# Experts of a MoE layer: three quarters of down in high and low parts, slots eight partitions apart, 8 KB weight pieces, three buffers for stored rows

## The reference

```python
idx, gw = route(h1)                  # 8 of 64 experts for each token, and their weights
for each expert e, rows = its tokens:         # 4352 rows over 64 experts, 68 on average
    h = silu(h1[rows] @ w_gate[e]) * (h1[rows] @ w_up[e])    # (n, 1024) @ (1024, 256)
    y = (h @ w_down[e]) * gate_weight                        # (n, 256) @ (256, 1024)
out = layer_norm(ALPHA * h1 + shared_swiglu(h1) + sum over a token's 8 experts of y)
```

## Time and profile before

| | |
|---|---|
| median of three runs | 1628.31 us (1626.76 to 1630.15) |
| profiled execution, whole | 1625.87 us |
| its span, first to last instruction | 1624.0 us |
| granted TensorE clock, mean over the span | 0.954 |
| busy: PE / DVE / ACT / POOL | 92% / 62% / 37% / 21% |
| bytes read from HBM and written | 301.33 MB and 42.12 MB |

### The profile page before, as it was taken

How to read it: one execution, slowest core, us unless ns; L and a number is a source line. 1 busy time by engine, 2 the same in 40 slices (tenths; PEclk the granted TensorE clock), 3 DMA queues, 4 the chain that set the end, 5 groups by cost and what they waited for, 6 DMA issues and landing times. The chain is left out here.

```text
span 1624.0 us, 20669 instructions
## 1 busy us (share of the span) xinstructions
PE 1494.0 (92%) x7986; PEld 1119.5 (69%) x7990; DVE 1006.1 (62%) x1713; ACT 601.9 (37%) x880; POOL 335.4 (21%) x233
## 2 busy tenths in 40 slices
PE   7999999979989985999997999999999999999654
PEld 6999999968888874444343777777766666677321
DVE  5649777245567664144554777777777777777276
ACT  3665333240230220000003555555555555555101
POOL 0000000022224221021230233333332221121024
PEclk9999999979999996999998999999999999999885
DMA  5222222200000002700074899999999999997392
GB/s 204 66 69 90 90 91 77 67 14 1 1 1 1 1 2 84 327 14 14 14 270 165 332 370 379 367 370 371 372 368 363 361 362 367 365 368 311 141 399 87
DMA packets 53159, 313.21 MB, mean 193 GB/s; under 512 B 14928, under 2 KB 15952, under 8 KB 34320
## 3 DMA queue, kind: packets, MB, share of 16 engines
q1 hardware_dynamic: 33312, 276.16, 44.6%
q0 software_dynamic: 19760, 35.89, 6.0%
HBM read 301.33 MB, written 42.12 MB: 211 GB/s over the span
## 5 line engine op out<-in xcount | busy, mean ns | idle before, releaser
L1880 DVE TENSOR_TENSOR gate_up_lo<-wide,gate_up_hi 128x2048 fp32r<-128x2048 f32 x128 | 293.1, 2291 | 92.2 <-ACT gate_up_hi L1823 91.6
L1823 ACT ACTIVATE gate_up_hi<-wide 128x2048 fp32r<-128x2048 f32 x128 | 244.6, 1913 | 7.4 <-PEq L1219 7.4
L302 PE MATMUL bank<-x_hi,w_hi 128*128 128x274 f32 x768 | 223.9, 291 | 0.0
L304 PE MATMUL bank<-x_hi,w_lo 128*128 128x274 f32 x768 | 223.0, 290 | 0.0
L303 PE MATMUL bank<-x_lo,w_hi 128*128 128x274 f32 x768 | 222.0, 289 | 0.0
L1751 PE MATMUL bank<-gate_up_hi,rows_hi 128*128 128x512 f32 x512 | 206.3, 403 | 7.7 <-DVE rows_lo L1889 7.7
L1753 PE MATMUL bank<-gate_up_hi,rows_lo 128*128 128x512 f32 x512 | 201.1, 393 | 0.0
L1752 PE MATMUL bank<-gate_up_lo,rows_hi 128*128 128x512 f32 x512 | 200.2, 391 | 0.0
L1689 POOL DMA_INDIRECT expert_rows<-lru,slot_ids x64 | 117.9, 1843 | 326.1 <-DVE lru L1896 312.5
L1771 PE MATMUL bank<-wide,zt 128*128 128x512 f32 x344 | 154.8, 593 | 1.0 <-DVE zt L1916 1.0
L302 PEld LDWEIGHTS bank<-x_hi,w_hi 128*128 128x128 f32 x768 | 144.9, 189 | 0.8 <-issue 0.5
(11 more groups left out here) (280 smaller groups left out, 2367.1 us busy)
## 6 DMA issues: line engine op xcount, KB each, us to landing
wide<-in_w_exp SPq DMA_DIRECT2D x64, 2048.0 KB
wide<-in_w_exp SPq DMA_DIRECT2D x43, 1024.0 KB, 12.8
w_raw<-in_w_in SPq DMA_DIRECT2D x48, 512.0 KB, 3.3
last_down<-in_w_exp SPq DMA_DIRECT2D x21, 1024.0 KB
expert_rows<-expert_rows SPq DMA_DIRECT2D x8, 2048.0 KB, 13.9
wide<-in_w_out SPq DMA_DIRECT2D x1, 3584.0 KB, 22.0
wide<-in_w_out SPq DMA_DIRECT2D x1, 2560.0 KB, 12.5
zt<-in_x_t SPq DMA_DIRECT2D x2, 1096.0 KB, 8.4
```

What stands on the lines that cost most here:

```text
L302: nc.tensor.matmul(out, wh[:, k, :], x_hi[:, k, at], start=(k == 0), stop=False)
L304: last = nc.tensor.matmul(out, wl[:, k, :], x_hi[:, k, at], start=False, stop=(k == DC - 1))
L1823: nc.scalar.activation(half(w_hi[b % 2], u), half(w_gu[b % RAW], u), ACT.Copy).then_inc(s_whi, 1)
L1880: nc.vector.tensor_tensor(half(w_lo[b % 2], u), half(w_gu[b % RAW], u), half(w_hi[b % 2], u), ALU.subtract).then_inc(s_wlo, 1)
```

## The change

Five edits. (1) Three of the four (row chunk, column half) units of down, `DN_UNITS`, are multiplied in parts; the fourth stays plain float32. For it hidden is split as well. Down is loaded as 1536 columns (6 KB a partition, two buffers) and 512 columns (2 KB, three buffers). ScalarE now writes both halves of y. (2) Rank 16i + g of an expert goes to partition 8g + i (`RANKS_APART` = 8), and `mem.ids` is read by eight DMAs. (3) The weights lie in HBM as two arrays; gate_up comes as two pieces of 8 KB for each partition, in one DMA. (4) y has three buffers. (5) The first expert's gate_up is split in quarters, with the rows' parts between them. Besides, constants that only the delta rule needs are a tensor of their own, which makes room. The core of the diff:

```diff
@@ loads @@
-    sp.dma_start(mem.w_gu[i], expert[:, 0:W_GU]).then_inc(mem.gu_loaded[i], 16)
-    sp.dma_start(mem.w_dn[i], expert[:, W_GU:W_EXP].rearrange("p (c n) -> p c n", c=FC)).then_inc(mem.dn_loaded[i], 16)
+DN_UNITS = ((0, 0), (0, 1), (1, 0))
+def load_gate_up(sp, mem, dram, b):
+    sp.dma_start(mem.w_gu[b % RAW].rearrange("p (h n) -> p h n", h=2), dram["w_gu"][b].rearrange("h p n -> p h n"))\
+        .then_inc(mem.gu_loaded[b % RAW], 16)
+def load_down(sp, mem, dram, b):
+    sp.dma_start(mem.w_dn[b % DN_RAW], dram["w_dn"][b, :, 0:DN_SPLIT]).then_inc(mem.dn_loaded[b % DN_RAW], 16)
+def load_down_whole(sp, mem, dram, b):
+    sp.dma_start(mem.w_dn_whole[b % RAW], dram["w_dn"][b, :, DN_SPLIT:]).then_inc(mem.dn_whole_loaded[b % RAW], 16)
@@ slots, in mixing_stage @@
-            pool.dma_start(mem.ids[:, :], dram["slots"].rearrange("(c p e) w -> c p (e w)", p=P, e=NE)[0])\
-                .then_inc(s_ids, 16)
+            by_rank = dram["slots"].rearrange("(c i g e) w -> c i g (e w)", i=RANKS_APART, g=P // RANKS_APART, e=NE)
+            for i in range(RANKS_APART):
+                pool.dma_start(mem.ids[i::RANKS_APART, :], by_rank[0, i]).then_inc(s_ids, 16)
@@ SyncE @@
-            for b in range(RAW - 2, NE):
-                if RAW <= b + 2 < NE:
-                    sp.wait_ge(s_wlo, 2 * (b + 2 - RAW) + 2)
+            gate_up(RAW)
+            gate_up(RAW + 1)
+            for b in range(DN_RAW, NE):
+                sp.wait_ge(s_dlo, b - DN_RAW + 1)
+                load_down(sp, mem, dram, b)
                 if b >= RAW:
                     sp.wait_ge(s_dn1, b - RAW + 1)
+                    load_down_whole(sp, mem, dram, b)
+                gate_up(b + RAW)
@@ TensorE, down @@
                     for c in range(FC):
-                        last = nc.tensor.matmul(mem.bank[4 + n][:, :], hidden_t[:, c, :],
+                        if (c, n) in DN_UNITS:
+                            unit = DN_UNITS.index((c, n))
+                            at = slice(512 * unit, 512 * unit + 512)
+                            nc.tensor.matmul(out, h_hi[:, c, :], d_hi[:, at], start=(c == 0), stop=False)
+                            nc.tensor.matmul(out, h_hi[:, c, :], d_lo[:, at], start=False, stop=False)
+                            last = nc.tensor.matmul(out, h_lo[:, c, :], d_hi[:, at], start=False, stop=(c == FC - 1))
+                        else:
+                            last = nc.tensor.matmul(out, hidden_t[:, c, :], w_dn_whole[b % RAW], start=False, stop=True)
@@ ScalarE, end of its loop @@
                 if b:
                     write_y(b - 1)
+                act.wait_ge(s_hdt, b + 1)
+                nc.scalar.activation(h_hi, mem.bank[6][:, 0:FC * P].rearrange("p (c i) -> p c i", c=FC), ACT.Copy)\
+                    .then_inc(s_hhi, 1)
+                split_down(b)
                 split(b + 2, 1)
@@ VectorE, its loop @@
                 split_rows(b + 1)
+                split(b + 1, 1)
                 split(b + 2, 0)
-                if b:
-                    write_y(b - 1)
-                dve.wait_ge(s_hdt, b + 1)
-                split(b + 2, 1)
+                split_hidden(b)
+                split_down(b)
```

More of the change, by code:

```diff
@@ L62 @@
 BIG = 1e30
+ROUTING = 2 * P + 2 + 5 * NE + NE * TILES + 2
 LEVELS = 7
@@ L67 @@
 _at = 0
-for _name, _n in (("ident", P), ("tri", P), ("before", P), ("ones", P), ("masks", LEVELS * P), ("future", P),
-                  ("experts", NE), ("valid", TILES + 1), ("row", 1), ("ln_eps", 1), ("over", TILES + 1),
+for _name, _n in (("ident", P), ("tri", P), ("before", P), ("ones", P), ("experts", NE), ("valid", TILES + 1), ("row", 1), ("ln_eps", 1), ("over", TILES + 1),
                   ("entries", (TILES + 1) * TOPK * 4)):
@@ L1187, in take @@
             nonlocal at
-            view = mem.carve(mem.states, at, *dims)
+            view = mem.carve(mem.routing, at, *dims)
             at += int(np.prod(dims))
@@ L1617, in expert_stage @@
         rows = mem.rows
-        act_g, hidden = (carve(mem.zt, D * ROWS + FF * i, FF) for i in range(2))
-        hidden_t = carve(mem.zt, D * ROWS + 2 * FF, FC, P)
-        y = [carve(mem.lru, D * i, D) for i in range(2)]
-        x_t = carve(mem.lru, 2 * D, DC, P)
+        y = [carve(mem.lru, D * i, D) for i in range(Y_ROWS)]
+        act_g, hidden = (carve(mem.lru, D * Y_ROWS + FF * i, FF) for i in range(2))
+        hidden_t = carve(mem.lru, D * Y_ROWS + 2 * FF, FC, P)
+        x_t = carve(rows[1], 0, DC, P)
+        h_hi, h_lo = (take(f"hidden_{n}", FC, P, dt=F32R) for n in ("hi", "lo"))
+        d_hi, d_lo = (take(f"down_{n}", DN_SPLIT, dt=F32R) for n in ("hi", "lo"))
         extra_ids = ctx.enter_context(nc.sbuf_tensor("extra_ids", [P, 4], U32))
@@ L1708, in _ @@
                 gather(b + 2 * ROWS)
-            for i in range(2):
-                pool.wait_ge(s_out[i], 16 * (NE // 2))
+            for i in range(Y_ROWS):
+                pool.wait_ge(s_out[i], 16 * len(range(i, NE, Y_ROWS)))
             pool.sem_inc(s_xfree, 1)
             def extra(i):
-                pool.wait_ge(s_xload, i * 48 + 48)
+                pool.wait_ge(s_xload, i * 64 + 64)
                 pool.sem_inc(mem.passed, 1)
@@ L1747, in up @@
                 for k in range(DC):
-                    if k % 4 == 0:
-                        pe.wait_ge(s_wlo, 2 * b + k // 4 + 1)
+                    if b == 0 and k % 2 == 0:
+                        pe.wait_ge(s_wlo, k // 2 + 1)
+                    elif k % 4 == 0:
+                        pe.wait_ge(s_wlo, splits(b - 1) + k // 4 + 1)
                     at = slice(512 * k, 512 * k + 512)
@@ L1807, in extra @@
                     for c in range(FC):
-                        last = nc.tensor.matmul(mem.bank[4 + n][:, :], hidden_t[:, c, :],
-                                                w_dn[0][:, c, 512 * n:512 * n + 512], start=(c == 0), stop=(c == FC - 1))
+                        unit = FC * c + n
+                        weights = w_dn[0][:, 512 * unit:512 * unit + 512] if (c, n) in DN_UNITS else w_dn_whole[0]
+                        last = nc.tensor.matmul(mem.bank[4 + n][:, :], hidden_t[:, c, :], weights,
+                                                start=(c == 0), stop=(c == FC - 1))
                 last.then_inc(s_xdn, 1)
@@ L2087, in constant_tables @@
 def constant_tables():
-    c = np.zeros((P, N_CONSTS), np.float32)
+    c, d = np.zeros((P, N_CONSTS), np.float32), np.zeros((P, N_DELTA_CONSTS), np.float32)
     def put(name, value):
-        at, n = CONSTS[name]
-        c[:, at:at + n] = value
+        table, out = (CONSTS, c) if name in CONSTS else (DELTA_CONSTS, d)
+        at, n = table[name]
+        out[:, at:at + n] = value
     p, q = np.arange(P)[:, None], np.arange(P)[None, :]
```

153 lines of the change are left out of this document (95 added, 58 removed).

## The result

The changed kernel takes 1641.12 us (median of 4 runs, 1637.68 to 1642.3), the kernel before 1628.27 in the same comparison (4 runs, 1626.76 to 1630.15): a ratio of 1.0077, 95% interval 1.0065 to 1.009. It is slower by 12.9 us, where 8 us less were forecast, and the time lies outside the range of 1592 to 1632. The profiled execution took 1642.30 us, with a span of 1640.5.

A forecast was written before the change was run, and what follows sets the result against it. TensorE bounded the old kernel; the busiest DMA engines would bound the new. First new gate_up load 879.8 + 7 + 60 S, then 25.5 and 2.5, gave 1517.8 against 1525.26: -7.5 us, 1618.4 profiled, 1620 us median, range 1592 to 1632.

The forecast's parts named there:

- The bound: Expert stage: it moves from TensorE, 9.49 us an expert after the change, to the busiest DMA engines.
- The compute side: Expert stage: TensorE's period falls to 9.49 us, ScalarE needs 8.2 and VectorE 8.4 us, and nothing is late.
- The first rival: Rows spread over all 16 DMA engines, S = 8.97, TensorE stays the bound at 9.49 us: 1594 us, chance 0.20.
- S: Time of the busiest DMA engines for one expert: between 9.83 (packet estimate) and 10.17 us (landings), taken as 10.05.
- 8 KB pieces: Gate_up rows as two packets, down rows as 6 KB and 2 KB: bytes cost the same, no capacity added.
- The 2.5 us at the end: Loss priced at the stage's end, since rows now unsent when the last weights land would be sent before them.
- Slots eight apart: New slot layout: again eight engines with 8 rows each at 64 tokens, the busiest holding as much as before.
- The lead: gate_up's time from issue to read falls from 22.6 to 16.0 us; landings of 15 us just fit.
- the slower rival: Shorter lead: landings over 16 us stop ScalarE and engines run dry; 1635 us at S = 10.3, chance 0.15.
- Three y buffers: ScalarE's waits for a stored y vanish; worth nothing, since its idle time hid them from TensorE.
- The start: First expert in quarters: first up near 876.2, 3.7 us sooner, mostly not kept; eight slot-table reads cost nothing.
- theory G: From the follow-up runs: faster compute engines, or their more SBUF reads and writes, slow the loads; 1622 to 1628 with down plain.

The follow-up runs named there:

- a_apart4: The changed kernel with slots of an expert four partitions apart in place of eight: 1593.21 us, ratio 0.9794.
- b_dn62: The kernel before with down loaded by two DMAs, 6 KB and 2 KB a partition, in place of one: 1626.03 us, ratio 0.9997.
- a_p16: The changed kernel with gate_up stored and loaded as one 16 KB piece for each partition again: 1639.99 us, ratio 1.0079.
- b_p8: The kernel before with gate_up as two 8 KB pieces for each partition in one DMA: 1626.93 us, ratio 1.0.
- a_gu_late: The changed kernel with each gate_up load issued one down load later, about 5 us later in the period: 1664.01 us, ratio 1.0229.
- b_dn62_late: The kernel before with down in 6 and 2 KB and each gate_up issued right behind the down load, 5.4 us later: 1631.27 us, ratio 1.0029.
- a_gu_early: The changed kernel with gate_up's second low half split ahead of the rows' low parts on VectorE, releasing the next load earlier: 1637.15 us, ratio 1.0062.
- a_y2: The changed kernel with two buffers for stored rows in place of three: 1641.48 us, ratio 1.0093.
- a_apart1: The changed kernel with slots as before the change, rank r in partition r: 1649.33 us, ratio 1.0131.
- a_four: The changed kernel with all four units of down in parts, down loaded in one 8 KB piece, slots eight apart: 1639.29 us, ratio 1.0069.
- a_four_apart4: The changed kernel with all four units of down in parts, down in one 8 KB piece, and slots four apart: 1584.31 us, ratio 0.9717.

## Why the prediction failed, point by point

**The bound was named rightly.** That it moves from TensorE to the eight DMA engines that carry rows, and that slots eight apart leave them eight, is shown by a_apart4: only the slots differ, and the pace goes from 10.23 to 9.46, with TensorE at 100.

**The compute side was right.** TensorE's period of 9.49 is a_apart4's 9.46; ScalarE's 8.2 us is 0.824 x 9.46 = 7.8 there, VectorE's 8.4 is 0.871 x 9.46 = 8.2. Nothing was late. The first rival's 1594 is what a_apart4 takes, 1593.21; it needed the rows spread, which eight apart does not do.

**The step that failed is S, "I take 10.05".** By landings it was 10.40, above both bounds (9.83 and 10.17). Put into the sum of the prediction against the profile:

| term | predicted | measured |
|---|---|---|
| first new gate_up load | 879.8 | 882.52 |
| 7 + 60 S | 610.0 | 631.0 (to 1513.5) |
| last landing to the end of the last down | 28.0 | 29.1 |
| end of the last down | 1517.8 | 1542.6 |

Of 24.8 us, 21.0 are S, 2.7 the start and 1.1 the chain behind the last landing. The profiled execution came 23.9 above the 1618.4 forecast for it. Both bounds were taken from the bytes or from the old kernel's landings, as if the time of an expert's loads were a property of the loads. It is not: 10.02 or less in b_dn62, 10.17 in the kernel before, 10.40 here. And 10.17 was a mean over a growth that slows: in windows of 100 us from 900 on, the old kernel's down loads land after 8.8, 11.2, 12.6, 14.3 and 15.4 us.

With S = 10.40 the sum of the prediction gives 1620 + 60 x 0.35 = 1641 us, the measured median. That it fits so closely is luck in part: the 3.8 us of the other two terms are made up by the profiled execution, which lies 1.2 us above its median here and lay 2.4 below it before.

**8 KB pieces** at nothing in capacity: right (a_p16, b_p8). The 2.5 us at the end cannot be told apart in the 29.1.

**Slots eight apart, "the busiest engines hold as much as before"**: wrong in size. In the kernel they are worth 8 us (1649.33 to 1641.12), and the growth of the old kernel's landings falls from 7.4 us to 2.8. A likely reason, argued and not shown: before, the first 36 rows of an expert already fill one engine with eight of them (partitions 0 to 3 and 32 to 35); eight apart, that takes 53 (ranks 0, 4, 16, 20 and so on to 52), so that with fewer tokens the busiest engine has less.

**The lead, "while a backlog exists no engine idles"**: not safe to rely on. The issue came as I walked it: 10.5 us after the start of an up (1204.13, the up at 1193.59), against 10.1 forecast and 4.67 before. Landings of 20.1 us are over the 16.0 of lead, and ScalarE waits as the slower rival said; it gave 1635 at S = 10.3, and should have had the larger chance. But that this later issue is what raised S is argued and not shown. 5 us more cost another 0.33 us an expert (a_gu_late), and a late issue brought back growing landings in the old kernel (b_dn62_late); both put gate_up within 1.3 us of down, where the changed kernel keeps 4.3 us, nearly the old 4.6. And issuing it earlier gave 0.03 to 0.05 us an expert (a_gu_early).

**Three y buffers** at nothing: right (a_y2). **The start**: the first up comes 3.55 us after the first turned row, where it came 7.67 after it, so the quarters save 4.1 us, 3.7 forecast. The stage itself began 3 us later (875.60 against 872.64), and other executions of kernels alike up to there began up to 7 us apart (868.69 in a_apart4); with one read of the slot table in place of eight it began at 875.81 (a_apart1), so the reads are not the reason.

**What stays open.** Why S is 10.40 here and 10.17 in the kernel before. It is not the size of gate_up's pieces (a_p16), not the third y buffer (a_y2) and not the third load (a_four has two for an expert, at a pace of 10.21). Left are the later issue, two down buffers in place of three, the later issue of down itself, and the faster work of the other engines (theory G); no run separates them. Nor does one show why down in 6 and 2 KB keeps the old kernel's landings at 6.3 us, where 8 KB let them grow to 16.2, or how the engines lose time when gate_up comes right behind down.

## What to carry to other kernels

When the work of one engine is shortened and the loads are within a few per cent of it, first count what each DMA engine carries: rows that fill half the partitions can sit on half the engines, and here one number (slots four apart in place of eight) was worth 48 us, where the change as it was made cost 13. Take the map from a transfer that runs alone, seen in slices, and test the new layout on it before using it. And do not take a pace of loads from a kernel that hides them as what they will do when they are the bound: do not price a later issue at nothing because a backlog seems to cover it, and keep two large loads apart: in both runs in which gate_up was only moved to a later place, right behind down, the kernel got slower (by 23 and 5 us). When a run is meant to take one thing away, look at the issue times in its trace for what else moved.

## What the runs showed of the hardware beyond that

- The DMA share does not tell how full the engines are. It stands at 0.99 with 359 GB/s (changed kernel) and at 1.01 with 397 (a_apart4) in the same stretch; between such kernels GB/s and landings tell them apart.
- 403 GB/s, weights and rows together, were held over 100 us (a_four_apart4), with the engines still ahead of TensorE.
- Rows and weights trade waiting: a gather lands after 19.1 us in the kernel before, 10.0 with gate_up in 8 KB pieces (b_p8) and 11.2 with down in 6 and 2 KB (b_dn62), at the same time of the kernel.
